# GpSimd's three weight remainders per set of w_down become negated highs plus adding DMAs

## The chip, the cores and the metric

One core of one Trainium2 chip runs the whole program. The metric is device time in microseconds (us); runs of the kernel before and after the change are compared. Matrix products run on TensorE (PE), and VectorE (DVE), ScalarE (ACT) and GpSimd (POOL) prepare operands and empty PSUM. SyncE (SP) issues most loads. DMAs that add into their destination are issued from POOL's queue.

## The reference

Two transformer blocks follow each other on 512 tokens of width 1024, all in float32. What matters here is the end of the first block and the start of the second:

```
hid = h @ w_up                                   # 1024 -> 2 x 2816
hid = conv_general_dilated(hid, conv_w ...) + conv_b
a, b = split(hid)
x = x + rmsnorm((gelu(a) * b) @ w_down, g_post_ffn)     # w_down: 2816 x 1024
h = rmsnorm(x, attn_norm_w[l])                   # second block
proj = einsum('bld,de->ble', h, w_in[l])
```

## The kernel before

**Three products for one.** PE multiplies float32 in a reduced format (fp32r), so each operand is split into a high part and a low part, the remainder. `three` issues high*high, high*low and low*high. For a block of weights the high part is a copy by ACT (`give_hi`, in the set stage `set_high`), and the low part is raw minus high, by POOL (`split`, in two halves of 128x1024) or by DVE (`low`, `set_weight_low`).

**The set stage.** 2048 of w_down's 2816 rows are done in two sets (q = 0 and 1) of seven products each after Strassen's scheme, 14 in all, numbered v = 7q + n. The products are `A11 B11`, `A12 B21`, `S1 T1`, `S2 T2`, `S4 B22`, `S3 T3` and `A22 T4`. B are blocks of 512x512 weights, T are sums of blocks, A and S the same of the tokens. Each product is 24 matmuls: two token tiles of 12, and in each the four k-slices of the weights in turn, three matmuls each. `set_product` holds PE until the weights' low part, the tokens' low part and the PSUM bank are there.

**Who makes what in it.** SP loads the four B of a set into four raw places (`SET_LOADS`). A place of the second set is loaded when the product of the first set that used it last has its low part and the sums that read it are done. ACT makes the high parts two products ahead (`set_token_high`, then `set_high`), and copies some results out of PSUM (`set_copy`). DVE makes the token sums and token low parts, the weight low parts of n = 2, 3, 5, 6 (`VECTOR_LOW`), T2 (`set_weight_sum`), and adds results into `h_added` (`set_take`). POOL makes the weight low parts of n = 0, 1 and 4 (L953), and issues the adding DMAs (`set_sum`, L927), two halves each: T1 (B12 from HBM is added onto B11 in place), T3 (also from HBM) and T4 (from SBUF onto B21's place). In POOL's order T1 stands behind the low part of n = 0 and ahead of that of n = 1, T3 stands ahead of n = 2, and T4 ahead of the low part of n = 4, behind T2. T1 may begin only when the low part of n = 0 is complete, because it overwrites B11.

**The chain in a set.** T1 must have landed before `set_high` of n = 2. T2 is made on T1's place after the low part of n = 2. T4 is T2 added onto B21. Each engine runs its instructions in the order written.

**The boundary to the second block.** The last 768 rows of w_down are three units (`down1`). PE does the first alone, and the last two tile by tile (`last_two_L`): 24 matmuls for each of four token tiles. The transposes of the normalized rows (`h_transposes`, L1162) of tiles 0 and 1 stand between the two halves of tiles 2 and 3. Those of tiles 2 and 3 stand behind tiles 0 and 1 of the next phase, `kv_iq`, of 24 matmuls each. For each tile `boundary` runs step A (DVE adds PSUM onto `h_added`, ACT sums squares, DVE scales and adds onto x), step B (ACT sums squares of x, DVE writes `h_rows`) and step C (high and low part of the transposed rows). The steps are interleaved: A0, B0, A1, C0, B1, A2, C1, B2, A3, C2, B3, C3. Before the boundary ACT and DVE make the high and low parts of the two units of `kv_iq`.

Of the kernel before, what the change touches and what calls it, by code (L numbers as in the profile page):

```python
# [4 lines left out]
P = 128  # L5
D = 1024
S = 512
NT = S // P
# [288 lines left out]

SET_N = 7 * SETS
SET_RAW = ({"B11": 2, "B21": 3, "B22": 0, "B12": 1}, {"B11": 0, "B21": 2, "B22": 1, "B12": 3})
SET_LOADS = ("B11", "B21", "B22", "B12")  # L300
# [44 lines left out]
def two_blocks(nc: bass.Bass, a, out: bass.AP):  # L345
# [11 lines left out]
    with ctx:  # L357
# [261 lines left out]
        set_hi = sem("set_hi")  # L619
        set_lows = [sem("set_low_pool"), sem("set_low_dve")]  # L620
        set_started = sem("set_started")
# [47 lines left out]
        def await_set_loaded(engine, q, name):  # L669

            slot = SET_RAW[q][name]
            engine.wait_ge(set_loaded[slot], 32 * (q + 1))

        def await_set_low(engine, v):

            by_vector, n = set_low(v)
            engine.wait_ge(set_lows[by_vector], n)

# [198 lines left out]
        def _(pool):  # L877
# [55 lines left out]

            for v in range(SET_N):
                q, n = divmod(v, 7)
                if n == 1:
                    await_set_loaded(pool, q, "B11")
                    await_set_low(pool, 7 * q)
                    set_sum(q, "T1", set_block(q, 0, 1))
                elif n == 2:  # L940
                    await_set_loaded(pool, q, "B12")
                    set_sum(q, "T3", set_block(q, 1, 1))
                elif n == 4:
                    await_set_low(pool, 7 * q + 1)
                    await_set_sum(pool, q, "T2")
                    set_sum(q, "T4", set_raw[SET_RAW[q]["B11"]].rearrange("p (k n) -> p k n", k=4))
                if set_low(v)[0]:
                    continue
                hi, lo = set_slot(v)
                pool.wait_ge(set_hi, v + 1)  # L950
                for half in range(2):
                    c = slice(half * UNIT // 2, (half + 1) * UNIT // 2)
                    made = nc.gpsimd.tensor_tensor(lo[:, c], set_raw_of(v)[:, c], hi[:, c].bitcast(f32), ALU.subtract)  # L953
                made.then_inc(set_lows[0], 1)
            for u in range(U0["down1"], U0["kv_iq"]):
# [39 lines left out]
        def _(pe):  # L995
# [283 lines left out]
            def set_product(v):  # L1279
# [3 lines left out]
                l_hi, l_lo = set_a[v % 3]  # L1283
                await_set_low(pe, v)
                pe.wait_ge(set_a_lo, v + 1)
                for t in range(2):
# [6 lines left out]
                    tok = slice(t * P, (t + 1) * P)  # L1293
                    for kk in range(4):
                        first, last = three(ps[:, b, :], l_hi[:, kk, tok], l_lo[:, kk, tok], hi[:, kk, :], lo[:, kk, :],
                                            n in OPENS and kk == 0, kk == 3, n not in OPENS)
                        if t == 0 and kk == 0:
                            first.then_inc(set_started, 1)
# [221 lines left out]
        def _(act):  # L1520
# [25 lines left out]

            def boundary(kind, tin, tout):

                for which, tt in STEPS:
                    tok = slice(tt * P, (tt + 1) * P)  # L1550
                    rms_out.wait()
# [171 lines left out]
            def set_high(v):  # L1723
# [13 lines left out]
                else:  # L1737
                    act.wait_ge(set_started, max(w for w in range(v) if SET_W[w] == SET_W[v]) + 2)
                nc.scalar.activation(set_slot(v)[0], set_raw_of(v), ACT.Copy).then_inc(set_hi, 1)

# [60 lines left out]
            load_gain(1, a["attn_norm"])  # L1801
            for u in range(U0["down1"] + 1, U0["kv_iq"] + 2):
                if u == U0["kv_iq"]:
                    root_table()
                give_hi(u, started=True)
            boundary("summed", T0["down1"], T0["h3"])

# [229 lines left out]
        def _(dve):  # L2037
# [7 lines left out]

            def boundary(kind, tin, tout, post, pre):
                for which, tt in STEPS:
                    c = 2 * tt + (which == "B")
                    tok = slice(tt * P, (tt + 1) * P)
                    if which == "A" and kind == "summed":  # L2050
                        for half in range(2):
                            t = tin + 2 * tt + half
                            row = h_added[:, 4 * half:4 * half + 4, tok]
                            await_psum(dve, t)
                            V.tensor_tensor(row, row, bank(t).rearrange("p (k n) -> p k n", k=4),
                                            ALU.add).then_inc(evacuated[BANK[t]], 1)
                        rms_in.take()
# [356 lines left out]
            def set_weight_low(v):  # L2414

                hi, lo = set_slot(v)
                dve.wait_ge(set_hi, v + 1)
                V.tensor_tensor(lo, set_raw_of(v), hi.bitcast(f32), ALU.subtract).then_inc(set_lows[1], 1)

# [12 lines left out]
            for at_v in range(SET_N):  # L2432
# [7 lines left out]
                if n == 1:  # L2440
                    set_weight_sum(q)
                if at_v + 2 < SET_N:
                    set_token_low(at_v + 2)
                    if set_low(at_v + 2)[0]:
                        set_weight_low(at_v + 2)
                set_take(2 * at_v)
                if at_v == 2:
# [7 lines left out]
            low(U0["kv_iq"])  # L2455
            low(U0["kv_iq"] + 1)
            boundary("summed", T0["down1"], T0["h3"], 0, 1)


# [346 lines left out]
```

## Time and profile before

| | |
|---|---|
| three runs | 1568.96, 1569.16 and 1571.22 us, median 1569.16 |
| profiled execution | 1572.05 us, span 1570.2 us |
| mean granted TensorE clock | 0.996 |
| PE busy | 1544.6 us, 98% of the span |
| DVE, POOL, ACT busy | 958.8, 732.6 and 553.5 us |
| DMA on POOL's queue | 18.88 MB |

A matmul is in flight longer than the distance to the next one, so a busy PE can still lose time: the distance between starts shows it. In the timeline a bracket at the end of a row gives the idle time before it and what ended it.

### The profile page before, as it was taken

The page shows a single profiled execution, that of the slowest core. Times are in us where ns is not written, and L with a number is a line of the kernel's source. Part 1 is how long each engine was busy: PE and PEld are TensorE (multiplying, and loading weights), DVE is VectorE, ACT ScalarE, POOL GpSimd, SP SyncE. Part 2 cuts the span into 40 slices and gives each one's busy share as a digit, 9 for nine tenths or more (in the row PEclk, how much of TensorE's full clock was granted, in tenths as well). Part 3 has the DMA queues.
Part 4 walks back from the last instruction along what each step waited for, and adds up shares of the span by engine and source line. Part 5 has one row for each costly group of instructions (what it writes and reads, how often), then busy time and mean ns, then how long its engine had stood idle before and what let it go on. Part 6 is the DMA issues. An engine that isn't in the chain of part 4 may idle for free.

```text
span 1570.2 us, 19119 instructions
## 1 busy us (share of the span) xinstructions
PE 1544.6 (98%) x7447; PEld 1271.4 (81%) x7447; DVE 958.8 (61%) x1225; ACT 553.5 (35%) x772; POOL 732.6 (47%) x297
## 2 busy tenths in 40 slices
PE   9999999999999999999999999999999999999997
PEld 6887788888888988888877797887778988888886
DVE  5901589820074554456994578997764436585878
ACT  3012211210124433334643435226643343333444
POOL 5875189687772254455453001441125252645551
PEclk9999999999999999999999999999999999999999
DMA  6242023233224133335664031332124164536472
GB/s 228 81 134 81 1 94 101 75 114 108 87 101 134 54 82 106 101 87 161 161 161 142 29 107 54 108 83 52 29 81 143 45 188 114 165 85 192 89 188 81
DMA packets 137687, 165.87 MB, mean 106 GB/s; under 512 B 5720, under 2 KB 98952, under 8 KB 137609
## 3 DMA queue, kind: packets, MB, share of 16 engines
q1 hardware_dynamic: 127478, 141.05, 28.2%
q0 software_dynamic: 8256, 18.88, 6.8%
q10 hardware_dynamic: 1874, 4.85, 1.0%
q8 instruction: 55, 0.90, 0.3%
q14 instruction: 24, 0.19, 0.0%
HBM read 156.37 MB, written 2.10 MB: 101 GB/s over the span
## 4 chain that ended last, share of the span: by engine, by line
PE 79%; POOL 6%; issue 5%; DVE 5%; ACT 3%; DMA 1%; POOLq 0%; ACTq 0%; SPq 0%; DVEq 0%
PE ps L1005 24%; PE ps L1006 23%; PE ps L1007 23%; PE ps L1162 3%; PE ps L1237 2%; POOL w_lo L990 1%; POOL w_lo L895 1%; PE ps L1435 1%; PE ps L1225 1%; POOL w_lo L988 1%; PE ps L1452 1%; POOL tail_lo L990 1%; POOL w_hi L890 1%; PE ps L1327 1%; POOL tail_lo L988 0%
## 5 line engine op out<-in xcount | busy, mean ns | idle before, releaser
L895 POOL TENSOR_TENSOR w_lo<-raw,w_hi 128x1024 fp32r<-128x1024 f32 x150 | 381.7, 2566 | 459.2 <-ACT w_hi L1538 456.4
L1005 PE MATMUL ps<-hT_hi,w_hi 128*128 128x512 f32 (+1 forms) x848 | 325.2, 383 | 1.1 <-POOL w_lo L895 0.5
L1006 PE MATMUL ps<-hT_lo,w_hi 128*128 128x512 f32 (+1 forms) x848 | 323.7, 382 | 0.0
L1007 PE MATMUL ps<-hT_hi,w_lo 128*128 128x512 f32 (+1 forms) x848 | 323.7, 382 | 0.0
L890 POOL TENSOR_TENSOR w_hi<-raw,cells 128x2048 fp32r<-128x2048 f32 x35 | 129.6, 3702 | 126.4 <-PE ps L1005 125.2
L1005 PEld LDWEIGHTS ps<-hT_hi,w_hi 128*128 128x128 f32 x848 | 159.7, 188 | 34.8 <-issue 2.3
L1007 PEld LDWEIGHTS ps<-hT_hi,w_lo 128*128 128x128 f32 x848 | 159.7, 188 | 30.8
L1006 PEld LDWEIGHTS ps<-hT_lo,w_hi 128*128 128x128 f32 x848 | 159.7, 188 | 30.2
L1005 PE MATMUL ps<-w_hi,hT_hi 128*128 128x512 f32 (+2 forms) x400 | 151.6, 379 | 0.5 <-POOL w_lo L914 0.5
L1006 PE MATMUL ps<-w_lo,hT_hi 128*128 128x512 f32 (+2 forms) x400 | 150.1, 375 | 0.0
L1007 PE MATMUL ps<-w_hi,hT_lo 128*128 128x512 f32 (+2 forms) x400 | 150.0, 375 | 0.0
L1538 ACT ACTIVATE w_hi<-raw 128x2048 fp32r<-128x2048 f32 (+1 forms) x50 | 94.3, 1887 | 66.9 <-PE ps L1005 48.1
L1005 PEld LDWEIGHTS ps<-w_hi,hT_hi 128*128 128x128 f32 x400 | 75.3, 188 | 13.9 <-POOL w_lo L914 0.9
L1007 PEld LDWEIGHTS ps<-w_hi,hT_lo 128*128 128x128 f32 x400 | 75.4, 188 | 13.4
L1006 PEld LDWEIGHTS ps<-w_lo,hT_hi 128*128 128x128 f32 x400 | 75.4, 189 | 12.7
L2347 DVE SCALAR_TENSOR_TENSOR taps<-ps,conv,taps 128x511 f32<-128x511 f32 x44 | 33.0, 749 | 83.4 <-ACT taps L1707 83.4
L1707 ACT ACTIVATE taps<-ps,conv 128x512 f32<-128x512 f32 x44 | 34.1, 777 | 125.7 <-PE ps L1007 125.7
L988 POOL TENSOR_TENSOR w_lo<-raw_tail,w_hi 128x1024 fp32r<-128x1024 f32 x13 | 34.9, 2686 | 83.9 <-ACT w_hi L1971 83.9
L2113 DVE TENSOR_TENSOR w_lo<-raw,w_hi 128x1024 fp32r<-128x1024 f32 (+1 forms) x20 | 22.1, 1144 | 65.0 <-ACT w_hi L1538 65.0
L1005 PE MATMUL ps<-w_hi,a_hi 128*128 128x512 f32 x152 | 59.4, 391 | 1.2 <-DVE w_lo L2696 0.7
L1006 PE MATMUL ps<-w_lo,a_hi 128*128 128x512 f32 x152 | 59.1, 389 | 0.0
L1007 PE MATMUL ps<-w_hi,a_lo 128*128 128x512 f32 x152 | 59.1, 389 | 0.0
(415 smaller groups left out, 3199.6 us busy)
## 6 DMA issues: line engine op xcount, KB each, us to landing
raw<-in_w_in SPq DMA_DIRECT2D x86, 512.0 KB, 4.6
raw<-in_w_up SPq DMA_DIRECT2D x54, 512.0 KB, 4.9
raw<-in_w_down SPq DMA_DIRECT2D x30, 512.0 KB, 6.3
raw_tail<-in_w_up SPq DMA_DIRECT2D x22, 512.0 KB, 4.9
raw<-in_w_out SPq DMA_DIRECT2D x16, 512.0 KB, 4.1
raw_tail<-in_w_down SPq DMA_DIRECT2D x16, 512.0 KB, 5.3
raw<-in_w_down POOLq DMA_DIRECT2D x12, 512.0 KB, 9.0
raw<-in_w_ret_o SPq DMA_DIRECT2D x8, 512.0 KB, 4.1
```

What stands on the lines that cost most here:

```text
L890: nc.gpsimd.tensor_tensor(hi[:, 0:n], raw[:, s, 0:n], zero.broadcast_to([P, n]), ALU.add).then_inc(unit_hi, 1)
L895: nc.gpsimd.tensor_tensor(lo[:, c], raw[:, s, c], hi[:, c].bitcast(f32), ALU.subtract).then_inc(unit_split, 1)
L988: nc.gpsimd.tensor_tensor(lo[:, 0:UNIT // 2], tail_raw_of(v)[:, 0:UNIT // 2], hi[:, 0:UNIT // 2].bitcast(f32), ALU.subtract)
L990: nc.gpsimd.tensor_tensor(lo[:, UNIT // 2:UNIT], tail_raw_of(v)[:, UNIT // 2:UNIT], hi[:, UNIT // 2:UNIT].bitcast(f32), ALU.subtract).then ...
L1005: first = nc.tensor.matmul(dst, a_hi, b_hi, start=start, stop=False, skip_group_check=onto)
L1006: nc.tensor.matmul(dst, a_hi, b_lo, start=False, stop=False, skip_group_check=onto)
L1007: return first, nc.tensor.matmul(dst, a_lo, b_hi, start=False, stop=stop, skip_group_check=onto)
L1162: last = nc.tensor.transpose(ps[:, BANK[t], n * width:n * width + width], src, ident[0:k, 0:k])
L1237: last = nc.tensor.matmul(ps[:, BANK[t], nn * 256:nn * 256 + 256], sT[:, h % 2, mb, n0:n0 + P], v[:, mb, h * RET_DV:(h + 1) * RET_DV], sta ...
L1538: nc.scalar.activation(slot_of(u)[0][:, 0:n], raw[:, s, 0:n], ACT.Copy).then_inc(hi_given, 1)
L1707: nc.scalar.activation(taps[:, j % 2, c, :], bank(t + c), ACT.Identity, bias=conv[:, 3, bass.ds(col, 1)], scale=conv[:, 1, bass.ds(col, 1) ...
L2347: V.scalar_tensor_tensor(tap[:, 1:S], ps[:, BANK[t + c], 0:S - 1], conv[:, 0, bass.ds(col, 1)], tap[:, 1:S], ALU.mult, ALU.add).then_inc(l ...
```

## The change

The low parts of n = 0, 1 and 4 are no longer made by POOL. ACT makes minus the high part in two halves of 128x1024 and writes it where the low part belongs, and for each half POOL issues a DMA that adds the raw weights onto it. Each of the three products of a set has two semaphores of its own, one for each half. PE waits for the first half ahead of the first k-slice and for the second ahead of the third. POOL and SP wait for both halves where they waited for the low part before. `set_take` of the first tile of n = 5 is put ahead of the token and weight low parts of that turn. At the boundary DVE adds a tile out of PSUM (`sum_tile`) one step earlier, tile 0 ahead of everything and tile tt + 1 in step B of tile tt. The high and low part of the second unit of `kv_iq` are moved into the boundary, on ACT ahead of B0 and on DVE ahead of A1.

```diff
+BY_DMA = tuple(n for n in range(7) if n not in VECTOR_LOW)
...
+        def await_set_low_half(engine, v, half):
+            engine.wait_ge(set_low_dma[BY_DMA.index(v % 7)][half], 16 * (v // 7 + 1))
...
-                pool.wait_ge(set_hi, v + 1)
                 for half in range(2):
                     c = slice(half * UNIT // 2, (half + 1) * UNIT // 2)
-                    made = nc.gpsimd.tensor_tensor(lo[:, c], set_raw_of(v)[:, c], hi[:, c].bitcast(f32), ALU.subtract)
-                made.then_inc(set_lows[0], 1)
+                    pool.wait_ge(set_negated, 2 * (3 * q + BY_DMA.index(n)) + half + 1)
+                    pool.dma_start(lo[:, c], set_raw_of(v)[:, c],
+                                   accum_op=ALU.add).then_inc(set_low_dma[BY_DMA.index(n)][half], 16)
...
-                await_set_low(pe, v)
+                if n not in BY_DMA:
+                    await_set_low(pe, v)
...
                     for kk in range(4):
+                        if t == 0 and kk % 2 == 0 and n in BY_DMA:
+                            await_set_low_half(pe, v, kk // 2)
...
-                nc.scalar.activation(set_slot(v)[0], set_raw_of(v), ACT.Copy).then_inc(set_hi, 1)
+                hi, lo = set_slot(v)
+                nc.scalar.activation(hi, set_raw_of(v), ACT.Copy).then_inc(set_hi, 1)
+                if n in BY_DMA:
+                    act.wait_ge(set_hi, v + 1)
+                    for half in range(2):
+                        c = slice(half * UNIT // 2, (half + 1) * UNIT // 2)
+                        nc.scalar.activation(lo[:, c], hi[:, c].bitcast(f32), ACT.Copy, scale=-1.0).then_inc(set_negated, 1)
...
-            for u in range(U0["down1"] + 1, U0["kv_iq"] + 2):
+            for u in range(U0["down1"] + 1, U0["kv_iq"] + 1):
...
-            boundary("summed", T0["down1"], T0["h3"])
+            boundary("summed", T0["down1"], T0["h3"], late=[U0["kv_iq"] + 1])
...
+                    if (which, tt) == ("A", 1):
+                        for u in late:
+                            low(u)
...
+                    if which == "B" and kind == "summed" and tt + 1 < NT:
+                        sum_tile(tin, tt + 1)
...
+                if n == 5:
+                    set_take(2 * at_v)
                 if at_v + 2 < SET_N:
                     set_token_low(at_v + 2)
                     if set_low(at_v + 2)[0]:
                         set_weight_low(at_v + 2)
-                set_take(2 * at_v)
+                if n != 5:
+                    set_take(2 * at_v)
...
-            low(U0["kv_iq"] + 1)
-            boundary("summed", T0["down1"], T0["h3"], 0, 1)
+            sum_tile(T0["down1"], 0)
+            boundary("summed", T0["down1"], T0["h3"], 0, 1, late=[U0["kv_iq"] + 1])
```

## Rows read from the trace of the kernel before

**Rows 1.** The page's first part: busy time, share and instructions of each engine.
```profile
PE 1544.6 (98%) x7447; PEld 1271.4 (81%) x7447; DVE 958.8 (61%) x1225; ACT 553.5 (35%) x772; POOL 732.6 (47%) x297
```
**Rows 2.** Timeline of PE in the set stage: start, duration, line, tiles, idle before.
```profile
752.89 0.39 PE L1005 MATMUL ps<-set_hi,set_a_hi 128*128 128x512 f32 x1
...
788.40 0.47 PE L1005 MATMUL ps<-set_hi,set_a_hi 128*128 128x512 f32 x1 [2.40 <-DVE h_added L2377]
...
790.45 0.63 PE L1005 MATMUL ps<-set_hi,set_a_hi 128*128 128x512 f32 x1
790.87 0.63 PE L1006 MATMUL ps<-set_lo,set_a_hi 128*128 128x512 f32 x1
...
829.42 0.39 PE L1005 MATMUL ps<-w_hi,set_a_hi 128*128 128x512 f32 x1
...
834.86 0.39 PE L1005 MATMUL ps<-w_hi,f_hi 128*128 128x512 f32 x1
```
**Rows 3.** Timeline of DVE in the set stage.
```profile
760.09 1.21 DVE L2404 SCALAR_TENSOR_TENSOR f<-f 128x1024 f32<-128x1024 f32 x1
761.23 2.28 DVE L2384 TENSOR_TENSOR set_raw<-set_raw,raw 128x2048 f32<-128x2048 f32 x1
...
784.25 3.40 DVE L2411 TENSOR_TENSOR set_a_lo<-f,set_a_hi 128x1024 fp32r<-128x1024 f32 x1
787.57 1.27 DVE L2377 TENSOR_TENSOR h_added<-h_added,ps 128x512 f32<-128x512 f32 x2
```
**Rows 4.** Stretches: PE, PEld, DVE, ACT, POOL busy, granted clock, DMA share, GB/s.
```profile
786.00:793.00 7.00, 4.60 (x13) 3.68 (x14) 7.00 (x6) 2.86 (x2) 6.41 (x5) 0.76 0.32 104
...
752.90:834.90 82.00, 78.97 (x338) 63.91 (x337) 72.65 (x54) 45.63 (x39) 41.15 (x22) 0.98 0.62 156
```
**Rows 5.** Timeline of PE at the boundary: transposes of tiles 0 and 3.
```profile
863.27 1.09 PE L1162 MATMUL ps<-ident,h_rows 128*128 128x128 f32 x8 [3.76 <-DVE h_rows L2098]
...
889.23 1.09 PE L1162 MATMUL ps<-ident,h_rows 128*128 128x128 f32 x8 [1.69 <-DVE h_rows L2098]
```
**Rows 6.** Timeline of DVE at the boundary.
```profile
852.20 2.36 DVE L2113 TENSOR_TENSOR spare_lo_down<-raw,spare_hi_down 128x1024 fp32r<-128x1024 f32 x2 [1.59 <-ACT spare_hi_down L1538]
854.47 1.28 DVE L2055 TENSOR_TENSOR h_added<-h_added,ps 128x512 f32<-128x512 f32 x2
...
861.93 1.28 DVE L2098 SCALAR_TENSOR_TENSOR h_rows<-x,cells,gain 128x1024 f32<-128x1024 f32 x1
```
**Rows 7.** Timeline of ACT in the set stage.
```profile
737.50 1.91 ACT L1739 ACTIVATE set_hi<-set_raw 128x2048 fp32r<-128x2048 f32 x1
...
765.36 1.43 ACT L1707 ACTIVATE taps<-ps,conv 128x512 f32<-128x512 f32 x2
...
780.88 1.06 ACT L1753 ACTIVATE set_a_hi<-f 128x1024 fp32r<-128x1024 f32 x1 [2.59 <-PE ps L1005]
```
**Rows 8.** Timeline of POOL around product 7.
```profile
783.83 6.05 POOL L953 TENSOR_TENSOR w_lo<-raw,w_hi 128x1024 fp32r<-128x1024 f32 x2 [9.06 <-ACT w_hi L1739]
790.47 2.46 POOL L927 DMA_DIRECT2D raw<-in_w_down  x2 [0.59 <-POOL w_lo L953]
```
**Rows 9.** L927 from 764 to 766 us: issues (ns, first and last start), landing.
```profile
L927 POOL DMA_DIRECT2D set_raw<-set_raw x2: 901/1062/1222, 764.1 to 764.7; - x2
...
DMA to landing us min/median/max: 4.6/5.6/6.6
```
**Rows 10.** L971, the same adding DMA elsewhere, four issued in a row.
```profile
L971 POOL DMA_DIRECT2D raw<-in_w_down x2: 1223/1465/1707, 1363.7 to 1364.5; - x2
L971 POOL DMA_DIRECT2D raw_tail<-in_w_down x2: 2209/2464/2718, 1365.2 to 1365.9; - x2
...
DMA to landing us min/median/max: 6.3/9.1/11.8
```
**Rows 11.** L807, SP's load of the second set's first block.
```profile
L807 SPq DMA_DIRECT2D raw<-in_w_down x2: 368/420/472, 774.8 to 775.2; - x2
...
DMA to landing us min/median/max: 4.0/4.5/4.9
```

More of the change, by code:

```diff
@@ L619, in two_blocks @@
         set_hi = sem("set_hi")
-        set_lows = [sem("set_low_pool"), sem("set_low_dve")]
+        set_low_dma = [[sem(f"set_low_dma{n}_{half}") for half in range(2)] for n in range(3)]
+        set_low_dve = sem("set_low_dve")
+        set_negated = sem("set_negated")
         set_started = sem("set_started")
@@ L672, in await_set_loaded @@
             engine.wait_ge(set_loaded[slot], 32 * (q + 1))
+        def await_set_low_half(engine, v, half):
+            engine.wait_ge(set_low_dma[BY_DMA.index(v % 7)][half], 16 * (v // 7 + 1))
         def await_set_low(engine, v):
             by_vector, n = set_low(v)
-            engine.wait_ge(set_lows[by_vector], n)
+            if by_vector:
+                engine.wait_ge(set_low_dve, n)
+            else:
+                for half in range(2):
+                    await_set_low_half(engine, v, half)
         def await_set_sum(engine, q, name):
@@ L1545, in root_table, with boundary @@
                 step.up(nc.scalar.activation(sq[:, 1:2], eps, ACT.Sqrt))
-            def boundary(kind, tin, tout):
+            def boundary(kind, tin, tout, late=()):
                 for which, tt in STEPS:
+                    if (which, tt) == ("B", 0):
+                        for u in late:
+                            give_hi(u, started=True)
                     tok = slice(tt * P, (tt + 1) * P)
@@ L1738, in set_high @@
                     act.wait_ge(set_started, max(w for w in range(v) if SET_W[w] == SET_W[v]) + 2)
-                nc.scalar.activation(set_slot(v)[0], set_raw_of(v), ACT.Copy).then_inc(set_hi, 1)
+                hi, lo = set_slot(v)
+                nc.scalar.activation(hi, set_raw_of(v), ACT.Copy).then_inc(set_hi, 1)
+                if n in BY_DMA:
+                    act.wait_ge(set_hi, v + 1)
+                    for half in range(2):
+                        c = slice(half * UNIT // 2, (half + 1) * UNIT // 2)
+                        nc.scalar.activation(lo[:, c], hi[:, c].bitcast(f32), ACT.Copy, scale=-1.0).then_inc(set_negated, 1)
             def set_token_high(v):
@@ L2044, in _, with sum_tile, boundary @@
             V = nc.vector
-            def boundary(kind, tin, tout, post, pre):
+            def sum_tile(tin, tt):
+                for half in range(2):
+                    t = tin + 2 * tt + half
+                    row = h_added[:, 4 * half:4 * half + 4, tt * P:(tt + 1) * P]
+                    await_psum(dve, t)
+                    V.tensor_tensor(row, row, bank(t).rearrange("p (k n) -> p k n", k=4),
+                                    ALU.add).then_inc(evacuated[BANK[t]], 1)
+            def boundary(kind, tin, tout, post, pre, late=()):
                 for which, tt in STEPS:
+                    if (which, tt) == ("A", 1):
+                        for u in late:
+                            low(u)
                     c = 2 * tt + (which == "B")
                     tok = slice(tt * P, (tt + 1) * P)
+                    if which == "B" and kind == "summed" and tt + 1 < NT:
+                        sum_tile(tin, tt + 1)
                     if which == "A" and kind == "summed":
[L2051 to L2056, printed above, removed]
                         rms_in.take()
@@ L2417, in set_weight_low @@
                 dve.wait_ge(set_hi, v + 1)
-                V.tensor_tensor(lo, set_raw_of(v), hi.bitcast(f32), ALU.subtract).then_inc(set_lows[1], 1)
+                V.tensor_tensor(lo, set_raw_of(v), hi.bitcast(f32), ALU.subtract).then_inc(set_low_dve, 1)
             with dve.Fori(0, FS // 4) as i:
```

## Prediction

> **What bounds the kernel now.** I read the page first. PE is busy for 98% of the span [rows 1], so a change on another engine counts only where PE waits for it, and the timeline of PE around w_down is the next view. The distance between two starts tells more than busy time. Product 13 takes 834.86 - 829.42 = 5.44 us for 24 matmuls, 0.227 each. The 14 products take 834.86 - 752.89 = 81.97 us and at that pace would take 76.2, so **the set stage loses 5.8 us**. Most of it goes ahead of product 6, the start at 788.40: PE stands idle for 2.40 us, and then matmuls start 0.42 apart instead of 0.227 for about eight of them [rows 2]. That is 2.40 + 1.6, or 4 us.
>
> The timeline of DVE names the cause. The result of product 5 is taken at 787.57, behind a token low part at 784.25 that took 3.40 us [rows 3] while POOL worked at product 7's low part from 783.83 on [rows 8]; an operation of that size takes 1.2. In the view of stretches the granted clock is 0.76 from 786 to 793, a mixture of the two levels, 2.4 and 1.2 GHz, after an idle time of 2.40 [rows 4].
>
> The boundary loses more. PE waits 3.76 us for the rows of tile 0 and 1.69 for those of tile 3 [rows 5]. Ahead of the first wait DVE is late: tile 0 is added out of PSUM at 854.47, behind the low part of `kv_iq`'s second unit at 852.20 [rows 6], while PE finished tile 0 at 834.86 + 72 x 0.227 = 851.2.
>
> **The change part by part.** I work out where PE would stand without any wait, when each operand comes, and take the later.
>
> *Removed.* Twelve low halves of POOL, 5 to 6 us for a pair (product 7's take 6.05 [rows 8]). Their going ends DVE's stretched operations, but no PE wait other than product 6's hangs on those. `set_take`, moved ahead of product 7's token low part, ends product 6's wait by itself: its result is there three quarters of a product after product 5 begins.
>
> *Added.* For each of six products ACT makes two negated halves and POOL issues two DMAs. A half costs ACT 1.05 us, as an operation of the same size does at 780.88 [rows 7]. The DMA is the disputed price, and no row shows this one. The nearest is T4, added from SBUF with the same size: the first half lands 4.6 us after its issue, the second at 764.7 + 6.6, which is 7.2 after the first issue [rows 9]. Where four halves are issued in a row, the first lands after 6.3 and the last at 1365.9 + 11.8, 14.0 after the first issue. That is 2.56 us for each further half [rows 10], so adding halves do not overlap; they stand in line. An old low part was complete some 5.5 us after its high part, and the new one needs 0.1 + 1.05 + 7.2 = 8.35.
>
> The Trainium skill has another price: in DMA: Bandwidth & Descriptors, Anatomy of one DMA, a DMA from GpSimd costs 2.0 us and its bytes over 436 GB/s. By that a half of 512 KB would hold the engines for 1.2 us, an estimate from that page, where the row has 2.56 for adding halves. The sum goes by the row.
>
> *The first set.* Product 0's high part is made from 737.50 to 739.41 [rows 7]. Its pair is issued from 740.5 and lands by 747.7; B12's load is under way, for which I add 0.6. T1 may not begin before that: 748.4. T1's second half lands 6.3 + 2.56 = 8.9 later, at 757.3, and product 1's pair, queued behind it, at 759.8 and 762.4. PE reaches the seventh matmul of product 1, where the second half is needed, at 752.89 + 5.44 + 1.36 = 759.7. So it waits 2.7.
>
> T1 at 757.3 leads on by a chain that each engine runs in order: high part of product 2 (1.95 with its semaphore), low part (2.3), a token sum (1.15, DVE 760.09), T2 (2.25, DVE 761.23 [rows 3]), high part of product 3 (1.95), two centre taps (1.4, ACT 765.36 [rows 7]), a token high part (1.0), high part of product 4 (1.9), one negated half (1.05), the pair (7.2). That is 22.15, and product 4's low part is complete at 779.4. Without waits PE is at product 4's seventh matmul at 776.0. **PE is 3.4 us late there**, product 1's wait included.
>
> *The second set.* Its first block goes where product 4's weights lay, so SP loads it from 779.5 on. That takes 775.2 + 4.9 - 774.8 = 5.3 us [rows 11], to 784.8. ACT waits for PE to begin product 5 at 783.5, makes a token high part from 784.0 and product 7's high part from 785.1 to 787.0. Product 7's pair is issued at 788.1 and lands by 795.3 if the DMA engines are free. They are not quite: before, SP's four loads kept them busy from 774.8 to about 788.2 (0.32 of 786 to 793 is 2.2 us [rows 4]), 13.4 us; starting at 779.5 they last to 792.9, and the pair's data starts 2 us after its issue, at 790.1. With equal shares the pair loses up to 2.8, with none 0. No row decides, so I take the middle, 1.4: 796.7. Behind its landing stand T1's two halves and then product 8's pair, four in a row: 796.8 + 14.0 = 810.8. PE without waits is at product 8's seventh matmul at 752.89 + 8 x 5.44 + 1.36 = 797.8. **PE is 13.0 us late there**, 9.6 more than at product 4. After such a wait I count a further 0.8 for matmuls at the lower clock; the rest of the eight fall into the wait for the second half.
>
> The Trainium skill says in DMA: Bandwidth & Descriptors, Queues, rings and completion order, that each DMA engine turns from queue to queue packet by packet. By that SP's loads and the pair share evenly, and the sum would be 1.4 us higher.
>
> Behind product 8 nothing is late: product 10's low part hangs on T2 and T2 on product 9's, both DVE's, with over 1 us to spare, and product 11's pair comes within 0.2 of PE. So the set stage loses 13.0 + 0.8 = 13.8 us instead of 5.8: **+8.0**. Product 6's wait is gone from this sum and nothing is won by it, since PE only comes earlier to product 8.
>
> *The boundary* (in the times of before; it hangs on PE). With the late unit out of the way DVE adds tile 0 as PSUM allows, to 852.2 instead of 855.75, and the rows of tile 0 are done at 863.21 - 3.55 = 859.7. PE is free at 859.5, so the wait of 3.76 goes. The moved low part (2.36 [rows 6]) now stands between tile 0's rows and step A of tile 1. DVE then has 2.36, two reciprocals (0.4) and five operations of 128x1024 at 1.2 to 1.3 (scale, add, low part C, the sums of tile 2, the gain): 9.0 us, to 868.7. PE wants tile 1's rows at 859.7 + 0.85 + 5.44 = 866.0. **A wait of 2.7 takes the place of that of 3.76**, and as after 2.40 us at product 6 I expect the lower clock, 1.5. Then come 0.85 + 36 matmuls, tile 2's transposes at 879.2, another 0.85 + 5.44, and tile 3's at 885.5 without a wait. Before, they began at 889.23 [rows 5]: **-3.7**. ACT's moved high part (1.9) fits into its wait for DVE's addition onto x, nearly 3 us.
>
> The sum is 8.0 - 3.7 = +4.3 us on the profiled execution, whose 1572.05 us stand 2.9 and whose span of 1570.2 stands 1.0 above the median of 1569.16. I carry the difference over to the median: **1573.5**.
>
> **The rivals.**
> *Adding halves pass like plain loads* (the other side). SP's halves land 1.3 apart [rows 11]. At that pace T1 lands by 754.1, product 4's pair by 775.0, before PE comes; product 7's is complete by 790.6, and product 8's at 790.7 + 6.3 + 3 x 1.3 = 800.9, only 3.1 late. Set stage -2.7, boundary -3.7: 1562.8. In the sum seven halves follow one another, three up to product 4 and four up to product 8: it comes out level at about 2.0 us a half, and 3 us faster at 1.5. For it: the source lies in SBUF. Against it: so did T4's, and its halves are 2.6 apart [rows 9]. By the 1.2 us for a half from the Trainium skill (DMA: Bandwidth & Descriptors, above) this rival would hold.
> *The small terms fall well.* No sharing at product 7 (-1.4) and no lower clock at tile 1 (-1.5): +1.4, 1570.6. For it: a single idle time of 2.40 [rows 2] is all that shows the clock falling after so short a wait. Against it: the one expected is longer.
> *The DMA engines become the bound.* They are busy for 0.62 of 82 us, 51 us [rows 4]; twelve halves of 2.56 add 31. No gap is left, and loads and pairs delay each other: equal sharing at product 7 (+1.4) and one half more, 2.6, on the way to product 4: +8.3, 1577.5. For it: that share. Against it: SP's loads and the adding DMAs mostly take turns, because both hang on the same low parts.
>
> **How the numbers follow.** Forecast 0.45, its own range 1570.7 to 1576.2; plain-load pace 0.14; small terms 0.22; bound by DMA 0.19. A difference under 0.2%, 3.1 us, can't be told from none. From the forecast I put 0.36 slower and 0.09 same, from the small terms 0.20 same and 0.02 slower, from the pace 0.13 faster and 0.01 same, from the DMA bound 0.19 slower. Faster 0.13, same 0.30, slower 0.57. The range 1564.5 to 1579 leaves out the ends of the first and last rival.
>
> **What would show it.** Right: PE's longest wait in the set stage ahead of product 8, 7 us or more, released by a DMA; adding halves 2.5 apart; no wait at product 6; tile 0's transposes without a wait, tile 1's with 2 to 3 us. Wrong: halves landing within 2.0 of each other, or product 8 starting within 3 us of product 7's end; or a wait behind product 9, where I see none.

## Result and profile after

The median goes from 1569.41 us (1568.96 to 1571.22) to **1584.05 us** (1582.98 to 1586.07). The ratio is 1.0092, with an interval of 1.008 to 1.0104: slower, as forecast, but by 14.6 us where the forecast had 4.3, and above the upper end of its range. The profiled execution took 1583.31 us with a span of 1581.4.

In the changed kernel `three` is L1015 to L1017, the transposes L1172, ACT's high part of a product's weights L1756 and its negated halves L1761. POOL's sums of blocks are L937, its new pairs L963. The page's first part answers to [rows 1]:

```profile
PE 1546.2 (98%) x7447; PEld 1271.8 (80%) x7447; DVE 944.6 (60%) x1225; ACT 565.4 (36%) x784; POOL 710.1 (45%) x297
```

DVE and POOL are busy for 14 and 22 us less, and the kernel is slower. The timeline of PE in the set stage answers to [rows 2]:

```profile
761.02 0.47 PE L1015 MATMUL ps<-w_hi,set_a_hi 128*128 128x512 f32 x1 [2.97 <-DMA w_lo<-set_raw]
...
764.13 0.80 PE L1015 MATMUL ps<-w_hi,set_a_hi 128*128 128x512 f32 x1 [1.34 <-DMA w_lo<-set_raw]
764.72 0.63 PE L1016 MATMUL ps<-w_lo,set_a_hi 128*128 128x512 f32 x1
765.15 0.63 PE L1017 MATMUL ps<-w_hi,set_a_lo 128*128 128x512 f32 x1
...
800.29 0.47 PE L1015 MATMUL ps<-w_hi,set_a_hi 128*128 128x512 f32 x1 [2.22 <-DMA w_lo<-raw]
...
814.24 0.76 PE L1015 MATMUL ps<-w_hi,set_a_hi 128*128 128x512 f32 x1 [7.21 <-DMA w_lo<-set_raw]
...
835.83 0.47 PE L1015 MATMUL ps<-w_hi,set_a_hi 128*128 128x512 f32 x1 [1.87 <-DVE h_added L2407]
...
853.28 0.39 PE L1015 MATMUL ps<-w_hi,f_hi 128*128 128x512 f32 x1
```

The set stage runs from 752.44 to 853.28: 100.84 us instead of 81.97, so it loses 24.7 instead of 5.8. The places are product 1 (7.4: two waits, one for each half, and matmuls 0.43 apart instead of 0.227), products 7 and 8 (14.1) and product 11 (3.2). The wait at product 11 bears the name of DVE, whose addition at L2407 ended at 835.79. But product 11 waits for an earlier one of that line (that of product 9's first tile, done by 830.6), and the first half of its own pair landed at 835.69, 0.14 ahead of the start: it is the DMA. Product 6's wait is gone.

The view of stretches answers to the second line of [rows 4]; the columns are the same:

```profile
752.44:853.28 100.84, 83.67 (x337) 66.03 (x336) 60.88 (x54) 53.56 (x47) 26.62 (x24) 0.92 0.83 189
764.10:769.30 5.20, 5.17 (x12) 4.09 (x13) 4.36 (x3) 3.25 (x3) 1.77 (x2) 0.51 1.12 208
```

The DMA engines go from 0.62 to 0.83 busy. In the second stretch PE has just stood idle for 2.97 and then for 1.34 us, the granted clock is 0.51, the lower of the two levels (1.2 GHz), and 12 matmuls take 5.2 us instead of 2.7.

What the chain of low parts did shows in the timeline of ACT, whose high parts wait for the loads and sums, and in the timeline of POOL, as in [rows 7] and [rows 8]:

```profile
771.18 1.06 ACT L1775 ACTIVATE set_a_hi<-f 128x1024 fp32r<-128x1024 f32 x1 [1.90 <-PE ps L1015]
772.15 1.90 ACT L1756 ACTIVATE w_hi<-raw 128x2048 fp32r<-128x2048 f32 x1
...
789.41 1.92 ACT L1756 ACTIVATE w_hi<-raw 128x2048 fp32r<-128x2048 f32 x1 [0.83 <-DMA raw<-in_w_down]
...
811.59 1.91 ACT L1756 ACTIVATE set_hi<-raw 128x2048 fp32r<-128x2048 f32 x1 [9.67 <-DMA raw<-in_w_down]
823.40 1.92 ACT L1756 ACTIVATE w_hi<-raw 128x2048 fp32r<-128x2048 f32 x1 [7.24 <-PE ps L1015]
```
```profile
775.44 1.81 POOL L963 DMA_DIRECT2D w_lo<-raw  x2 [7.05 <-ACT w_lo L1761]
792.72 1.80 POOL L963 DMA_DIRECT2D w_lo<-raw  x2 [15.47 <-ACT w_lo L1761]
803.21 2.44 POOL L937 DMA_DIRECT2D raw<-in_w_down  x2 [8.69 <-DMA w_lo<-raw]
804.66 2.80 POOL L963 DMA_DIRECT2D w_lo<-set_raw  x2
```

These are the high parts of products 4, 7, 9 and 10, and the issues of product 4's pair, product 7's pair, T1 of the second set and product 8's pair. L963 by itself, in stretches around three of its pairs (product 4, product 7, product 8), gives the landings, as [rows 9] and [rows 10] do for the sums:

```profile
L963 POOL DMA_DIRECT2D w_lo<-raw x2: 856/856/856, 775.4 to 776.4; - x2
...
DMA to landing us min/median/max: 4.6/5.4/6.2
...
L963 POOL DMA_DIRECT2D w_lo<-raw x2: 856/857/858, 792.7 to 793.7; - x2
...
DMA to landing us min/median/max: 7.4/8.2/9.0
...
L963 POOL DMA_DIRECT2D w_lo<-set_raw x2: 1912/2082/2251, 804.7 to 805.2; - x2
...
DMA to landing us min/median/max: 9.4/10.7/12.0
```

Alone, a pair's first half lands after 4.6 us and its second at 776.4 + 6.2, 7.1 after the first issue, as T4 had shown. Beside SP's loads product 7's pair needs 9.9. Behind T1 product 8's pair ends at 805.2 + 12.0 = 817.2, 14.0 after T1's issue.

The transposes of the boundary answer to [rows 5]:

```profile
878.01 1.09 PE L1172 MATMUL ps<-ident,h_rows 128*128 128x128 f32 x8
886.72 1.09 PE L1172 MATMUL ps<-ident,h_rows 128*128 128x128 f32 x8 [2.14 <-DVE h_rows L2128]
895.86 1.04 PE L1172 MATMUL ps<-ident,h_rows 128*128 128x128 f32 x8
902.19 1.03 PE L1172 MATMUL ps<-ident,h_rows 128*128 128x128 f32 x8
```

From the end of the set stage to tile 3's transposes it takes 902.19 - 853.28 = 48.91 us instead of 54.37: the moves at the boundary give back 5.5 in these two profiles.

### The profile page after: what moved, and what is told of

It reads as the page before. It is cut to its first block, busy times and chain, and to the rows that moved or that the text cites. A ratio compares the mean times of both kernels' runs of the same rounds, so it can differ in the third digit from the quotient of the medians.

```text
span 1581.4 us, 19132 instructions
## 1 busy us (share of the span) xinstructions
PE 1546.2 (98%) x7447; PEld 1271.8 (80%) x7447; DVE 944.6 (60%) x1225; ACT 565.4 (36%) x784; POOL 710.1 (45%) x297
## 4 chain that ended last, share of the span: by engine, by line
PE 79%; POOL 6%; issue 4%; DMA 4%; DVE 3%; ACT 3%; POOLq 0%; SPq 0%; DVEq 0%; ACTq 0%
PE ps L1015 24%; PE ps L1017 23%; PE ps L1016 23%; PE ps L1172 3%; PE ps L1247 2%; DMA w_lo<-set_raw 2%; DMA w_lo<-raw 1%; POOL w_lo L1000 1%; PE ps L1448 1%; POOL w_lo L905 1%; PE ps L1235 1%; POOL w_lo L998 1%; PE ps L1465 1%; POOL tail_lo L1000 1%; POOL w_hi L900 1%
## 5 line engine op out<-in xcount | busy, mean ns | idle before, releaser
L1015 PE MATMUL ps<-hT_hi,w_hi 128*128 128x512 f32 (+1 forms) x848 | 324.6, 383 | 1.1 <-POOL w_lo L905 0.5
L1017 PE MATMUL ps<-hT_hi,w_lo 128*128 128x512 f32 (+1 forms) x848 | 323.2, 381 | 0.0
L1015 PEld LDWEIGHTS ps<-hT_hi,w_hi 128*128 128x128 f32 x848 | 159.4, 188 | 34.6 <-issue 2.3
L1017 PEld LDWEIGHTS ps<-hT_hi,w_lo 128*128 128x128 f32 x848 | 159.4, 188 | 30.7
L1015 PE MATMUL ps<-w_hi,hT_hi 128*128 128x512 f32 (+2 forms) x400 | 151.5, 379 | 0.3 <-POOL w_lo L924 0.3
L1017 PE MATMUL ps<-w_hi,hT_lo 128*128 128x512 f32 (+2 forms) x400 | 150.1, 375 | 0.0
L1015 PEld LDWEIGHTS ps<-w_hi,hT_hi 128*128 128x128 f32 x400 | 75.3, 188 | 13.8 <-POOL w_lo L924 0.7
L1017 PEld LDWEIGHTS ps<-w_hi,hT_lo 128*128 128x128 f32 x400 | 75.4, 188 | 13.3
L1015 PE MATMUL ps<-w_hi,a_hi 128*128 128x512 f32 x152 | 59.4, 391 | 1.1 <-DVE w_lo L2729 0.7
L1017 PE MATMUL ps<-w_hi,a_lo 128*128 128x512 f32 x152 | 59.1, 389 | 0.0
```

The source lines that it names most:

```text
L1015: first = nc.tensor.matmul(dst, a_hi, b_hi, start=start, stop=False, skip_group_check=onto)
L1017: return first, nc.tensor.matmul(dst, a_lo, b_hi, start=False, stop=stop, skip_group_check=onto)
```

## Experiments

**First group.** The question was which part costs. One theory, called the line, was that only the queue of adding halves costs: where a pair stands behind T1. The first run takes all adding DMAs and ACT's negated halves back and keeps the moves (`BY_DMA` empty, POOL subtracts again; only the line that decides it is shown):

```diff
-BY_DMA = tuple(n for n in range(7) if n not in VECTOR_LOW)
+BY_DMA = ()
```

> The kernel after, but GpSimd makes the three low parts of each set by subtraction again; the moved set_take and the moved steps of the boundary stay. Theory (the line): all of the loss comes from low parts that land late because adding halves stand in line. Then the set stage loses 5.8 - 4 = about 2 us, the boundary keeps its gain of 5.5, and the time is 1558 to 1562. Rival (moved steps): part of the loss comes from the moves on VectorE and ScalarE; then 1566 or more. The rival about ScalarE (its negated halves push the high parts back) also gives 1558 to 1562 here and is told apart by the kernel that keeps them.

Measured: 1566.91 us, ratio 0.9981 [0.9972, 0.9991]. So the new low parts, negated halves and adding DMAs together, cost 17.1 us, and the moves gain 2.6, less than the line expected. The time lies in the range of the rival that a move costs something. The timeline of PE shows where the rest went:

```profile
797.37 0.50 PE L1026 MATMUL ps<-w_hi,set_a_hi 128*128 128x512 f32 x1 [0.90 <-POOL w_lo L968]
...
812.12 0.50 PE L1026 MATMUL ps<-w_hi,set_a_hi 128*128 128x512 f32 x1 [3.07 <-DVE w_lo L2459]
```

Product 6 no longer waits, and product 10, whose row is the second, starts at 812.12, where it started at 812.14 before. Something other than PE sets product 10's time.

The second run does the opposite: the kernel before, with the adding DMAs and without the moves.

> The kernel before with the low parts by adding DMAs alone: set_take and the boundary as before. Theory (the line): the set stage loses as much as after the whole change, since TensorE comes late to product 6 anyway, and the boundary's 5.5 us come back: 1588 to 1591. Rival (moved steps cost): under 1584.

Measured: 1588.02 us, ratio 1.012 [1.0103, 1.0137], as expected by the line.

The third sets the pair of n = 1 ahead of T1 in POOL's order:

```diff
 for v in range(SET_N):
     q, n = divmod(v, 7)
     if n == 1:
+        add_raw(v)
         await_set_loaded(pool, q, "B11")
...
-    for half in range(2):
...
+    if n in (0, 4):
+        add_raw(v)
```

> The kernel after, but in GpSimd's order the adding pair of n = 1 stands ahead of T1 instead of behind it. Theory (the line): no wait at product 8 on its low part over 2 us, since its pair no longer stands behind T1; T1 lands 5 us later against its pair instead, so that waits appear at products 2 and 9 on VectorE's low parts; in sum 1577 to 1582. Rival (the transfers of a pair are slow in themselves, wherever they stand): product 8 still waits 5 us or more for its DMA and the time is 1584 or more.

Measured: 1588.64 us, ratio 1.0121 [1.0104, 1.0138]. The places came as the line expected, the time did not (1577 to 1582). With the pair of n = 1 ahead of it, T1 lands later, and the waits turn up behind it. In the timeline of PE these are products 2 and 9:

```profile
768.88 0.80 PE L1020 MATMUL ps<-w_hi,set_a_hi 128*128 128x512 f32 x1 [5.16 <-DVE w_lo L2453]
...
821.26 0.50 PE L1020 MATMUL ps<-set_hi,set_a_hi 128*128 128x512 f32 x1 [4.06 <-DVE set_lo L2453]
```

The fourth keeps ACT's negated halves, lets POOL subtract only after both, and uses no adding DMA, so that the negated halves are written and overwritten (two lines of it; the rest is as in the first run):

```diff
+pool.wait_ge(set_negated, 2 * sum(w % 7 in BY_POOL for w in range(v + 1)))
 made = nc.gpsimd.tensor_tensor(lo[:, c], set_raw_of(v)[:, c], hi[:, c].bitcast(f32), ALU.subtract)
```

> The kernel after with ScalarE's negated halves kept, but GpSimd then writes the low parts over them by subtraction, once both halves are done; no adding pair. Theory (the line): 2.1 us later low parts at products 4 and 11, the only ones without slack: 1561 to 1565. Rival (ScalarE): the negated halves push the high parts and cost most of the loss: 1577 or more.

Measured: 1576.42 us, ratio 1.0045 [1.0028, 1.0062], between the two expectations. Some 2 us ahead of each low part cost 9.5 us more than the first run, though no DMA was added. The line can't explain that. Nor is all of the 17.1 the adding DMAs' own. How late a low part is can be read from the traces: product 7's is complete 6.2 us after its high part in the first run, 7.9 us here, and 11.3 us in the changed kernel. The timeline of PE has the waits at products 4, 8, 10 and 11:

```profile
778.82 0.79 PE L1026 MATMUL ps<-w_hi,set_a_hi 128*128 128x512 f32 x1 [3.82 <-POOL w_lo L968]
...
804.86 0.50 PE L1026 MATMUL ps<-w_hi,set_a_hi 128*128 128x512 f32 x1 [2.05 <-POOL w_lo L968]
...
819.67 0.50 PE L1026 MATMUL ps<-w_hi,set_a_hi 128*128 128x512 f32 x1 [2.05 <-DVE w_lo L2459]
...
827.91 0.50 PE L1026 MATMUL ps<-w_hi,set_a_hi 128*128 128x512 f32 x1 [2.50 <-POOL w_lo L968]
```

**A second theory: the chain.** In the trace of before the following steps follow one another: product 4's low part complete at 774.77, the load onto its place issued then and landed at 780.12, a token high part at 780.88, product 7's high part at 781.85 and its low part from 783.83 to 789.88, T1 issued 790.47 and landed 799.01, product 9's high part 799.03 and low part 800.98, T2, product 10's high part 807.84 and low part to 812.08, product 10 at 812.14. From product 7's high part on each step hangs on the one before it, with no gap over 0.6 us but one of 2.3 ahead of T2 (805.52), which stands behind additions and a token sum in VectorE's order. Ahead of product 7's high part there is a gap of 1.7 us: the load is there at 780.12, but ACT comes to that high part only behind the token high part at 780.88, which waits for PE to begin product 5 [rows 7]. The theory is that a later low part of n = 0, or one of n = 4 that is late by more than that gap, is handed on to product 10 in full; the low part of n = 1 is in no such chain. It also explains the third run of the first group: the pair that is put ahead of T1 puts itself into the chain, and product 9's high part begins at 816.97, against 811.59 in the changed kernel. The second group puts adding DMAs on one n at a time, with all moves kept and POOL subtracting for the others (only the deciding line is shown):

```diff
-BY_DMA = tuple(n for n in range(7) if n not in VECTOR_LOW)
+BY_DMA = (4,)      # in the others (0,), (1,), and (0, 4)
```

> The changed kernel with only the low parts of n = 4 (products 4 and 11) made by a negated high part and adding DMAs; n = 0 and n = 1 are GpSimd's subtraction again, the moves stay. Reference is the run in which all three are GpSimd's and the moves stay (1566.9). Chain theory: the low part of product 4 stands in the chain low part of 4, load into its buffer, high part of 7, low part of 7, and so on to product 10, which is back to back; the halves are in SBUF about 7.1 us after issue instead of a 6.05 us subtraction, with the negated halves and the load's sharing some 4 to 6 us more, handed on to the end: 1571 to 1573, and product 10 or 11 has the wait. Line theory (only the adding halves' queueing behind GpSimd's token sums costs, which is at products 1 and 8): no more than 1569.

> The changed kernel with only the low parts of n = 0 (products 0 and 7) made by a negated high part and adding DMAs; n = 1 and n = 4 are GpSimd's subtraction, the moves stay. Chain theory: the low parts of 0 and 7 both stand ahead of a token sum by DMA in the chain that ends at product 10; the low part of 7 comes 4 to 5 us later than by subtraction, and what product 0's costs is handed on to product 4's subtraction, so 1575 to 1578 against 1566.9 with none. Line theory: product 0 is made ahead of the stage and product 7 waits some 2 to 3 us, 1568 to 1571.

> The changed kernel with only the low parts of n = 1 (products 1 and 8) made by a negated high part and adding DMAs, which queue behind the token sum of the same set; n = 0 and n = 4 are GpSimd's subtraction, the moves stay. Chain theory: low(1) and low(8) are in no chain to product 10, TensorE's wait of 5 to 9 us at product 8 is for the greater part one that product 10 would have had anyway (3.1 us there without it), 1568 to 1571 against 1566.9 with none. Line theory: the halves behind the token sum are the cost, product 1 waits 3 to 7 and product 8 some 10 us, and the time is 1575 or more.

A kernel with two of them followed, to see whether the costs add:

> The changed kernel with n = 0 and n = 4 by adding DMAs and n = 1 by GpSimd's subtraction. Alone, n = 0 cost 6.3, n = 4 6.2 and n = 1 1.4 us above the run with none (1566.9), 13.9 together where all three cost 17.1. If n = 0's and n = 4's delays add along the chain and the missing 3 us come from product 1's wait, which only n = 1 behind a delayed token sum makes: 1578 to 1581. If n = 0 and n = 4 hinder each other (sharing of DMAs at product 7's halves): 1581.5 to 1584.

| low parts by adding DMAs | product 9's high part begins | set stage ends | median, us | ratio to before |
|---|---|---|---|---|
| none (first run) | 799.02 | 834.87 | 1566.91 | 0.9981 [0.9972, 0.9991] |
| n = 1 | 798.80 | 836.75 | 1568.28 | 0.999 [0.9981, 0.9999] |
| n = 4 | 801.81 | 843.26 | 1573.11 | 1.0023 [1.0014, 1.0032] |
| n = 0 | 806.06 | 841.87 | 1573.22 | 1.0024 [1.0014, 1.0034] |
| n = 0 and 4 | 809.83 | 849.19 | 1581.64 | 1.0071 [1.0057, 1.0085] |
| all | 811.59 | 853.28 | 1584.05 | 1.0092 [1.008, 1.0104] |

Against what was expected: n = 1 lies in the chain theory's range, n = 4 0.1 us above it, and n = 0 1.8 us below it. Both together came out in the range of the second hypothesis, that n = 0 and n = 4 hinder each other, 0.6 us above that of the first.

The second column, which tells how late the chain is, is read in the timeline of ACT. For n = 4:

```profile
801.81 1.92 ACT L1767 ACTIVATE set_hi<-raw 128x2048 fp32r<-128x2048 f32 x1 [7.27 <-DMA raw<-in_w_down]
```

for n = 0:

```profile
806.06 1.91 ACT L1767 ACTIVATE set_hi<-raw 128x2048 fp32r<-128x2048 f32 x1 [10.27 <-DMA raw<-in_w_down]
```

for both:

```profile
809.83 1.91 ACT L1767 ACTIVATE set_hi<-raw 128x2048 fp32r<-128x2048 f32 x1 [10.32 <-DMA raw<-in_w_down]
```

and for n = 1, with PE's wait at product 8 below it:

```profile
798.80 1.91 ACT L1767 ACTIVATE set_hi<-raw 128x2048 fp32r<-128x2048 f32 x1 [5.89 <-DMA raw<-in_w_down]
...
801.39 0.77 PE L1026 MATMUL ps<-w_hi,set_a_hi 128*128 128x512 f32 x1 [4.75 <-DMA w_lo<-set_raw]
```

The delays nearly add: 2.79 for n = 4, 7.04 for n = 0, 10.81 for both (9.83 by the sum). Of the further 1.0, 0.6 arises between the issue of product 7's pair and that of T1, 10.3 us with both and 9.7 with n = 0 alone. The gap ahead of product 7's high part counts too: with n = 4 the load ahead of it lands 4.5 us later than in the first run (784.38 against 779.88), and ACT begins product 7's high part 3.0 later, the 1.6 of the gap being used up. For n = 1 the chain is not late at all. PE waits 4.75 us at product 8 there, and product 10 follows without a wait, where the first run had 3.07: the kernel pays 1.4 us. By the line this run should have been the dearest; it is the cheapest, and the line is out as the main cause.

For n = 4 the delay at product 9 is only 2.79, and the set stage ends 8.4 later in the profile (the median is 6.2 higher; the profiled execution is the slowest of its eleven, 1.8 above their median). The rest is product 11, whose pair shares the DMA engines with the load for `down1`. PE waits for each half, and after the second it works at the lower clock for ten matmuls (granted 0.50 from 826.3 to 830.3):

```profile
822.49 0.47 PE L1026 MATMUL ps<-w_hi,set_a_hi 128*128 128x512 f32 x1 [1.84 <-DMA w_lo<-raw]
...
826.26 0.80 PE L1026 MATMUL ps<-w_hi,set_a_hi 128*128 128x512 f32 x1 [1.74 <-DMA w_lo<-raw]
```

**The moves apart.** Two kernels have one of the moves each, without adding DMAs: the boundary's alone, and product 6's `set_take` alone.

> The kernel before with only the boundary's moves (next tile's sums ahead of the second norm, the last high part at its tile 0 step and the last low part ahead of tile 1); product 6's token low part and evacuation stand in their old order, and all low parts are subtractions. Chain theory: what product 6 waits (2.4 us before) is swallowed at product 10 by the chain in either order, so the move of product 6's evacuation is worth nothing, and this runs like the kernel with all moves: 1566 to 1568. If that move has a worth of its own, this is 2 to 5 us above it: 1569 to 1572.

> The other half: the kernel before with only product 6's evacuation moved ahead of token low part of product 8; boundary and low parts as before. Chain theory: no difference from the kernel before, 1568.5 to 1570; product 10 has a wait of 3 us that stood at product 6. If the move has a worth of its own: 1565 to 1567.

Measured: 1565.73 us (0.9973 [0.9962, 0.9984]) and 1570.97 us (1.001 [1.0001, 1.0019]). Both lie just outside the ranges of the chain theory, by 0.3 and 1.0 us. The boundary's moves gain 3.8 us, and the move of `set_take` gains nothing: it costs 1.2 us beside the boundary's moves and 1.4 alone, about as much as the intervals are wide on either side. The wait goes from product 6 to product 10, and in the profile of the second kernel the clock falls after it:

```profile
811.93 0.80 PE L1026 MATMUL ps<-w_hi,set_a_hi 128*128 128x512 f32 x1 [3.06 <-DVE w_lo L2458]
```

**Shortening the chain.** If the chain binds, a faster link must help. Two kernels have all moves and only subtractions, and let VectorE make some of POOL's low parts (the deciding lines):

```diff
-    by_vector = [w % 7 in VECTOR_LOW for w in range(SET_N)]
+    by_vector = [w % 7 in VECTOR_LOW or w in SET_MORE for w in range(SET_N)]
...
+SET_MORE = (4, 7, 11)      # in the other kernel (7,)
```

> All low parts by subtraction, moves kept, but VectorE instead of GpSimd makes those of products 4, 7 and 11 (2.3 us instead of 6.05 us each). Chain theory: the chain that ends at product 10 loses two subtractions' difference, some 7 us, so that the 3.1 us at product 10 and most of what the set stage still loses go: 1561 to 1563 against 1566.9. If the chain isn't what bounds the stage, 1565 to 1568, since VectorE gets 7 us more work in it.

> All low parts by subtraction, moves kept, VectorE instead of GpSimd only for the one of product 7. Chain theory: the subtraction of 7 is a link of the chain to product 10 and the links ahead of it leave it some 2 us slack less, so 3.7 us shorter takes product 10's 3.1 us wait off: 1563 to 1565 against 1566.9. If links ahead (low part of 4, the load after it) hold the chain back as well, less: 1565 to 1567.

Measured: 1563.85 us (0.9961 [0.9948, 0.9975]) and 1562.78 us (0.996 [0.9946, 0.9973]). The first lies between its two ranges, the second 0.2 us below its first one. Both beat the kernel before and the changed one. With product 7's low part alone moved, product 9's high part comes 2.23 us earlier than in the first run, and product 10's wait falls from 3.07 to 0.60:

```profile
796.79 1.91 ACT L1768 ACTIVATE set_hi<-raw 128x2048 fp32r<-128x2048 f32 x1 [3.66 <-DMA raw<-in_w_down]
...
809.89 0.50 PE L1027 MATMUL ps<-w_hi,set_a_hi 128*128 128x512 f32 x1 [0.60 <-DVE w_lo L2460]
```

The set stage ends 2.23 us earlier, while the medians are 4.1 apart. In the profiles 1.6 us of the rest is the lower clock behind tile 1's transposes, which the first run has and this one has not; that part is not the chain's.

The links of products 4 and 11 in addition win nothing that the two intervals tell apart. For product 4 the trace shows why. Its low part is complete 2.5 us earlier (the load behind it is issued at 771.83 instead of 774.37), but ACT still waits for PE to begin product 5 ahead of product 7's high part:

```profile
780.07 1.06 ACT L1787 ACTIVATE set_a_hi<-f 128x1024 fp32r<-128x1024 f32 x1 [2.37 <-PE ps L1027]
```

So with subtractions the link that binds is product 7's low part and what follows it; product 4's enters only when it is late by more than the gap.

## Why the prediction went wrong

**What was right.** The direction; the price of a pair alone (7.2 forecast, 7.1 measured) and of a pair behind T1 (14.0 and 14.0), with halves that stand in line 2.6 us apart; the longest wait ahead of product 8; nothing won by product 6; no wait at tile 0's transposes and one of 2 to 3 us at tile 1's. The Trainium skill's price (DMA: Bandwidth & Descriptors, Anatomy of one DMA) would have put the halves some 1.2 us apart. The trace doesn't agree for an adding DMA, and the rival that went by plain loads fell with it.

**The step that failed** is the sum of the set stage: +8.0 forecast, +18.9 measured, 10.9 short. The mechanism, late low parts handed on from pair to load to pair, was the forecast's. But a term was put at nothing (what comes behind product 8), a dependency was missed (PE's own delay), and other terms were sized too small:
- *Behind product 8 nothing is late* was wrong: product 11 loses 3.2, the wait behind product 9 that the forecast had named as a sign against it. Product 10's high part needs the weight place of product 8, so ACT waits for PE to begin product 9 (the row at 823.40, 7.24 idle). Product 11's pair, issued at 829.46, then runs beside the load for `down1`, and its halves land after 6.2 and 8.7 us instead of 4.6 and 7.2.
- *Product 1 waits 2.7* was 7.4. Product 0's pair took 9.1 us beside B12's load instead of 7.8 (7.2 and 0.6), T1 was issued 0.6 us behind its landing and not at once, and so T1's issue and product 1's second half came 1.7 later than I had. The wait comes in two pieces, and the 12 matmuls after the second run at the lower clock, 2.5 us that I had not counted there. I also took the chain on to product 4 as free of PE. It is not: the token high part at 771.18 waits 1.90 us for PE's product 2. So PE's own delay enters the chain once more, and product 4's pair was complete at 782.58 instead of 779.4: 1.1 from T1 and 2.0 from this.
- *The load after it* was 5.3 us and took 6.8 (782.63 to 789.39). In the five runs in which product 4's pair lands just ahead of this load it took 5.8 to 6.9, in the other nine 5.2 to 5.5; why is not shown. *Sharing at product 7's pair* was a middle of 1.4 and came out at 2.7. That is the equal sharing of the third rival, and the rule of the Trainium skill that I cited (DMA: Bandwidth & Descriptors, Queues, rings and completion order) agrees: 9.9 us instead of 7.2. That rival's premise that no gap is left did not hold over the stage, where the DMA engines are busy for 0.83.
- T1 of the second set was therefore issued at 803.21 instead of 796.8, and 14.0 us on, product 8's second half was 6.4 late. The stage began 0.45 earlier. Matmuls at the lower clock after product 8 cost 1.6 instead of 0.8. 6.4 + 0.45 + 0.8 + 3.2 makes the 10.9.

**The boundary** was -3.7 and is -5.5. Tile 1's wait of 2.14 came, but without the lower clock that I had counted at 1.5. That part is luck, and what the second rival had: in the eleven profiles with these moves this wait is 2.13 to 2.15 us, and in five of them the matmuls behind it take 1.6 us longer, in six not.

**The carrying over** leaves a further 1.7. At tile 3's transposes the changed kernel is 12.96 us later in the profiles (902.19 against 889.23; 4.3 + 10.9 - 1.8, less the 0.45 of the earlier start), and the medians are 14.6 apart. The profiled execution of before stands 2.6 us above the median of its kernel (1572.05 against 1569.41), that of the changed kernel 0.7 below its own. Of the 2.6, 1.6 was lost outside both stages and by chance: from 1068 to 1086 us the granted clock was 0.91, which shows in no other of the fourteen profiles. A difference of stages leaves that out, as it should; the remaining 1.0 and the 0.7 were not traced. The forecast's remark that the span stands only 1.0 above the median compares a span with a device time; span with span it is 2.7 (1570.2 against 1567.5 us in the run of 1569.41).

Against which baseline does the change cost what? By the medians, one step after the other: the boundary's moves -3.8, `set_take` +1.2, negated halves with adding DMAs for n = 0 and n = 4 +14.7, for n = 1 a further 2.4. Their sum is 14.5.

What is not settled: by the medians n = 0 and n = 4 together cost 14.7 us, and one by one 12.5. In the profiles it is the other way about: the set stage ends 14.3 us later with both, and 8.4 and 7.0 with one. The profiled execution of both is the fastest of its five, 2.5 below their median, and that of n = 4 the slowest of its eleven. So whether the two hinder each other in the time, as they do by 1 us in the chain, is open. The intervals of these runs are about 1.5 to 2 us wide on either side.

## What to carry to other kernels

Before an operation is exchanged for one that frees a busy engine but takes longer, look for the chain of loads and sums that runs through it. It can be nearly back to back while each engine in it is half idle and the main engine waits for it only here and there; follow it from the late operand backward until a step has slack. In this kernel a gain on a wait ahead of the chain's end came back at that end, and a delay was handed on, less the slack, and paid again where the longer transfer met a load. One profiled execution can stand above or below the median of its kernel: carry over the difference of the stages that the change touches, and look for losses that belong to one execution alone.

## What the runs showed of the hardware

- A VectorE operation of 128x512, with both inputs in SBUF, took 6.21 us where it began beside POOL's subtraction, in the first run:

```profile
791.67 6.21 DVE L2407 TENSOR_TENSOR f_lo<-taps,f_hi 128x512 fp32r<-128x512 f32 x1
```

and 0.69 us in the run with products 4, 7 and 11 on VectorE, though POOL's subtraction for product 8 ran there too:

```profile
791.02 0.69 DVE L2408 TENSOR_TENSOR f_lo<-taps,f_hi 128x512 fp32r<-128x512 f32 x1
```

What differs is who was first. In the first run POOL's two halves ran from 791.63, 0.04 us ahead of VectorE's operation, to 797.32, and VectorE was done 0.6 us later. In the other run POOL began at 790.29, while VectorE was at an operation that it had begun at 789.88 and others followed without a gap, and there POOL was the late one:

```profile
791.63 5.69 POOL L968 TENSOR_TENSOR w_lo<-set_raw,w_hi 128x1024 fp32r<-128x1024 f32 x2
...
790.29 8.12 POOL L969 TENSOR_TENSOR w_lo<-set_raw,w_hi 128x1024 fp32r<-128x1024 f32 x2
```

The Trainium skill says so (SBUF — State Buffer, SBUF: two separate sides): a VectorE operation with two SBUF inputs and a GpSimd operation that reads SBUF want the same pair of ports, and the one that starts later stands still. The trace agrees in both runs, and the late one stood still over more than one instruction: VectorE over both of POOL's halves in the first; in the other POOL's first half took 4.81 us, while VectorE's operations ran on to 792.84.

- The length of a wait alone did not tell whether the clock falls. After 2.14 us idle ahead of tile 1's transposes the granted clock over the next 36 matmuls was 1.00 in the changed kernel and 0.84 in the first run, 1.6 us dearer; it fell so in five of the eleven profiles with this wait. After 3.07 and 3.06 us ahead of product 10 it was 1.00 in the first run and 0.73 in the kernel with `set_take` alone (812 to 818 us).
